# A two-block transformer kernel: rotation products moved to GpSimd, fetches of the second mixer reordered, matmuls in array halves interleaved

## What is computed

```python
h = x + nsa_mixer(rmsnorm(x), ...)          # attention: compressed, selected and windowed keys, 16 heads of 64
h = h + s5_mixer(rmsnorm(h), ...)           # second mixer, below
x = rmsnorm(h, final_norm)
# second block: retention, gated linear attention and sliding-window attention (window 128, 16 heads),
# merged by gates, w_out, then a gated FFN
```

```python
u, z = split(h @ w_in)
x[t] = A * x[t-1] + B @ u[t]                # complex, A = exp(lambda dt), per group
y[t] = Re(C @ x[t]) + d * u[t];  y = gelu(y)
ga, gb = split(y @ w_glu);  out = (ga * sigmoid(gb) * silu(z)) @ w_out
```

## Time and profile before

| | us |
|---|---|
| runs | 2107.24, 2108.03, 2109.11 (median 2108.03) |
| profiled execution, time / span | 2107.77 / 2106.0 |
| TensorE (PE) busy | 1864.1 (89%) |
| DVE busy | 1022.7 (49%) |
| ACT busy | 818.4 (39%) |
| POOL busy | 266.2 (13%) |
| chain that ended last | PE 70%, DVE 17%, ACT 6%, DMA 4%, SP's queue 2% |

### The profile page before, as it was taken

One profiled execution on the slowest core, in us unless ns is written; L12 is line 12 of the kernel. 1 busy time (PEld: TensorE's weight loads), 2 busy tenths in 40 slices (PEclk: granted clock), 3 DMA queues, 4 the chain that ended last, 5 costly groups with the idle time before them and its releaser, 6 DMA issues.

```text
span 2106.0 us, 23601 instructions
## 1 busy us (share of the span) xinstructions
PE 1864.1 (89%) x9454; PEld 1466.5 (70%) x9454; DVE 1022.7 (49%) x1731; ACT 818.4 (39%) x1348; POOL 266.2 (13%) x338
## 2 busy tenths in 40 slices
PE   3478689998976899899799999999999959999996
PEld 2366578776754787687477776887778738888885
DVE  7757855664535436523434544434444354443323
ACT  4024356763213424423434555345542342323222
POOL 0327633540000000000000000012210020111000
PEclk9789899999997999999999999999999979999998
DMA  3153331006774332221132222221122203222331
GB/s 105 66 181 114 103 116 43 12 2 182 175 188 109 117 100 70 100 98 43 40 101 88 80 71 70 93 70 61 51 71 90 90 20 110 92 98 91 99 92 58
DMA packets 80893, 187.56 MB, mean 89 GB/s; under 512 B 24576, under 2 KB 35712, under 8 KB 78992
## 3 DMA queue, kind: packets, MB, share of 16 engines
q1 hardware_dynamic: 80784, 186.06, 28.2%
HBM read 167.68 MB, written 18.35 MB: 88 GB/s over the span
## 4 chain that ended last, share of the span: by engine, by line
PE 70%; DVE 17%; ACT 6%; DMA 4%; SPq 2%; issue 2%; POOL 0%; DVEq 0%; ACTq 0%; POOLq 0%
PE bank L827 17%; PE bank L829 16%; PE bank L828 16%; DVE wlo L1723 2%; PE bank L1008 2%; PE bank L986 2%; PE bank L868 2%; PE bank L866 2%; PE bank L867 2%; PE bank L1199 1%; PE bank L1223 1%; DVE CA L1691 1%; PE bank L847 1%; PE bank L848 1%; PE bank L849 1%
## 5 line engine op out<-in xcount | busy, mean ns | idle before, releaser
L827 PE MATMUL bank<-Hh,whi 128*128 128x512 f32 (+1 forms) x1248 | 503.7, 404 | 27.4 <-DVE wlo L1723 18.2
L828 PE MATMUL bank<-Hl,whi 128*128 128x512 f32 (+1 forms) x1248 | 491.1, 393 | 0.0
L1723 DVE TENSOR_TENSOR wlo<-wraw,whi 128x1024 fp32r<-128x1024 f32 (+1 forms) x262 | 324.2, 1241 | 343.4 <-ACT whi L1250 341.9
L829 PE MATMUL bank<-Hh,wlo 128*128 128x512 f32 (+1 forms) x1248 | 490.9, 393 | 0.0
L1250 ACT ACTIVATE whi<-wraw 128x1024 fp32r<-128x1024 f32 (+1 forms) x262 | 271.2, 1040 | 401.2 <-PE bank L829 273.4
L827 PEld LDWEIGHTS bank<-Hh,whi 128*128 128x128 f32 (+1 forms) x1248 | 236.3, 189 | 92.0 <-DVE wlo L1723 14.8
L829 PEld LDWEIGHTS bank<-Hh,wlo 128*128 128x128 f32 (+1 forms) x1248 | 235.9, 189 | 52.8 <-issue 0.3
L828 PEld LDWEIGHTS bank<-Hl,whi 128*128 128x128 f32 (+1 forms) x1248 | 236.6, 190 | 51.7 <-issue 2.2
L2460 POOL TENSOR_SCALAR bs<-dist 128x256 f32<-128x256 f32 x16 | 7.7, 479 | 900.1 <-DMA dist<-in_c_dist 899.3
L827 PE MATMUL bank<-Bh,whi 128*128 128x512 f32 x256 | 103.7, 405 | 2.2 <-DVE Bl L2253 2.2
L829 PE MATMUL bank<-Bh,wlo 128*128 128x512 f32 x256 | 102.2, 399 | 0.0
(11 more groups left out here) (356 smaller groups left out, 2891.2 us busy)
## 6 DMA issues: line engine op xcount, KB each, us to landing
wraw<-in_w_o SPq DMA_DIRECT2D x24, 512.0 KB, 3.5
wraw<-in_w_bgate SPq DMA_DIRECT2D x24, 512.0 KB, 3.5
wraw<-in_w_branch SPq DMA_DIRECT2D x24, 512.0 KB, 3.5
wraw<-in_w_fg SPq DMA_DIRECT2D x22, 512.0 KB, 3.5
wraw<-in_w_fu SPq DMA_DIRECT2D x22, 512.0 KB, 3.5
wraw<-in_w_s SPq DMA_DIRECT2D x16, 512.0 KB, 3.5
wraw<-in_w_glu SPq DMA_DIRECT2D x16, 512.0 KB, 3.5
wraw<-in_w_fd SPq DMA_DIRECT2D x16, 512.0 KB, 3.5
```

The lines of the kernel that those rows point to most:

```text
L827: pe.matmul(o, wh[:, cols], hi(k), start=k == 0, stop=False)
L828: pe.matmul(o, wh[:, cols], lo(k), start=False, stop=False)
L829: m = pe.matmul(o, wl[:, cols], hi(k), start=False, stop=k == K - 1)
L1723: dve.tensor_tensor(c.wlo[q][:, 0:n], c.raw[i % RR][:, 0:n], c.whi[q][:, 0:n].bitcast(F32), S_).then_inc(*up(DID, ("wlo", i)))
```

## The change

1. The rotations are made on GpSimd (POOL), after attention, in SBUF where they stay (`Rt`, [128, 4, 2, 8, 64]); no DRAM copy, no fetch `mR`. DVE waits for the event `Rt` before the fifth u tile and in `states`. `prep` has six ticks less. The memsets of `kl` no longer stand behind the round trip.
2. Fetches of `mW` (`w`) and of `mCA`/`mT` (`m`) are letters of the order string.
3. The halves of y are made block by block (`y`), in memory of their own (`Yh`, `Yl`); those of the gated result right behind each `glu`.
4. `outputs`: all T matmuls first, before the wait for `Xs`, then all CA matmuls. `gla_o`: all At first, then all St.
5. `rsT` behind the first gemm of the next block, `final_norm` behind the row gemms of `w_rv`.
6. Sliding window: scores of two units are made together, matmuls of the two row halves in turn, in banks of their own; outputs of two units likewise in column halves, one step later; `pTs` has four buffers.

```diff
         self.attention()
+        for m in range(6):
+            self.step("prep_r", m)
         self.pair([("w_o0", 0), ("w_o0", 1)], "g0")
...
-                if b == 0:
-                    self.step("prep_r", n)
-                    yield
-            if b == 0:
-                self.step("prep_rout")
...
-        fns = dict(u=u_tile, r=rows, s=states, o=outputs, t=turned, z=z_tile, f=finish)
-        order = ("u0 u1 r0 u2 u3 r1 s0 u4 u5 r2 o0 s1 u6 u7 r3 t0 o1 s2 z0 z1 f0 t1 o2 s3 z2 z3 f1 t2 o3 z4 f2 t3 z5 "
-                 "z6 z7 f3")
+        def split_y(b):
+            for k in (2 * b, 2 * b + 1):
+                self.step("split_y", k)
+
+        def fetch_w(b):
+            self.step("fetch_w", b)
+
+        def fetch_m(b):
+            self.step("fetch_m", b)
+        fns = dict(u=u_tile, r=rows, s=states, o=outputs, t=turned, z=z_tile, f=finish, y=split_y, w=fetch_w, m=fetch_m)
+        order = ("u0 u1 r0 u2 u3 r1 s0 u4 w1 u5 r2 o0 s1 u6 w2 m2 u7 r3 t0 o1 s2 z0 w3 z1 m3 f0 t1 o2 s3 y0 z2 z3 f1 y1 "
+                 "t2 o3 z4 f2 y2 t3 z5 z6 z7 f3 y3")
         for s in order.split():
             fns[s[0]](int(s[1]))
-        self.step("hold", "y")
-        for k in range(KT):
-            self.step("split_y", k)
+        self.step("hold", "h2")
         self.pair([("w_glu", 0), ("w_glu", 8)], "y")
         for k in range(KT):
...
                 self.gemm("w_r", h, "h2")
-            self.evict(("w_r", h))
-        for h in range(4):
-            self.gemm("w_r", 4 + h, "h2")
-            self.evict(("w_r", 4 + h))
+            if h == 2:
+                self.bank.take("rsT")
+                self.step("rsT")
+                self.bank.give("rsT")
+                self.evict(("w_r", 0))
+                self.evict(("w_r", 1))
+            if h > 1:
+                self.evict(("w_r", h))
         self.rows_v("w_rv")
+        for k in range(KT):
+            self.step("final_norm", k)
         self.side = self.gate_tiles("w_rg")
...
-        for i in range(n + 3):
+        for i in range(n + 4):
+            if i < n and i % 2 == 0:
+                for jj in range(2):
+                    for u in (i, i + 1):
+                        self.bank.take(("ws", u, jj))
+                        self.bank.give(("ws", u, jj))
+                self.step("ws", i)
             if i < n:
-                stage_a(i)
+                self.step("wa", i)
             self.tick()
             if 1 <= i <= n:
                 self.step("wb", i - 1)
-            if i >= 3:
-                stage_d(i - 3)
+            if i >= 4 and i % 2 == 0:
+                self.bank.take(("wo", i // 2 - 2))
+                self.step("wd", i - 4)
+                self.bank.give(("wo", i // 2 - 2))
             if 2 <= i <= n + 1:
-                stage_c(i - 2)
+                for m in range(2):
+                    self.bank.take(("wp", i - 2, m))
...
+        halves = [slice(0, 64), slice(64, 128)]
+        ys = [bank(("y", b, i)) for i in range(2)]
+        for i in range(2):
+            on.wait_ge(*before(plan.bank, ("y", b, i)))
         on.wait_ge(*at("mats", b))
+        for q in range(8):
+            cols = slice((q % 4) * 128, (q % 4) * 128 + 128)
+            for h in range(2):
+                pe.matmul(ys[q // 4][halves[h], cols], c.U[b][:, 2 * q + h, :], T[:, 2 * q + h, :],
+                          start=(q % 4 == 0), stop=False, skip_group_check=True)
         on.wait_ge(*at("xs", b))
-        for i in range(2):
-            y = bank(("y", b, i))
-            on.wait_ge(*before(plan.bank, ("y", b, i)))
-            for q in range(4 * i, 4 * i + 4):
-                cols = slice((q % 4) * 128, (q % 4) * 128 + 128)
-                halves = [slice(0, 64), slice(64, 128)]
+        for q in range(8):
+            cols = slice((q % 4) * 128, (q % 4) * 128 + 128)
+            for part in range(2):
                 for h in range(2):
-                    pe.matmul(y[halves[h], cols], c.U[b][:, 2 * q + h, :], T[:, 2 * q + h, :],
-                              start=True, stop=False, skip_group_check=True)
-                for part in range(2):
-                    for h in range(2):
-                        x = pe.matmul(y[halves[h], cols], c.Xs[b % 2][halves[h], part, q, :],
-                                      CA[halves[h], part, q, 1:9, :].rearrange("p k n -> p (k n)"),
-                                      start=False, stop=(part == 1), skip_group_check=True)
-            x.then_inc(*up(PE, ("y", b, i)))
+                    x = pe.matmul(ys[q // 4][halves[h], cols], c.Xs[b % 2][halves[h], part, q, :],
+                                  CA[halves[h], part, q, 1:9, :].rearrange("p k n -> p (k n)"),
+                                  start=False, stop=(part == 1), skip_group_check=True)
+            if q % 4 == 3:
+                x.then_inc(*up(PE, ("y", b, q // 4)))
 
     def turned(b):
...
+        o = [bank(("go", h, t // 2))[:, (t % 2) * 256:(t % 2) * 256 + 256] for t in range(4)]
         for t in range(4):
-            o = bank(("go", h, t // 2))[:, (t % 2) * 256:(t % 2) * 256 + 256]
             for p in range(2):
-                pe.matmul(o[halves[p], :], c.At[halves[p], t, :], c.gv[halves[p], t, h * 256:h * 256 + 256],
-                          start=True, stop=(t == p == 0), skip_group_check=True)
-            for p in range(2):
-                n = 2 * t + p
-                if n:
-                    on.wait_ge(*at("St", h, n - 1))
-                    x = pe.matmul(o[halves[p], :], q[:, n * 64:n * 64 + 64], c.St[:, n - 1, :],
-                                  start=False, stop=True, skip_group_check=True)
-            if t % 2:
-                x.then_inc(*up(PE, ("go", h, t // 2)))
+                pe.matmul(o[t][halves[p], :], c.At[halves[p], t, :], c.gv[halves[p], t, h * 256:h * 256 + 256],
+                          start=(t % 2 == 0), stop=(t == p == 0), skip_group_check=True)
+        for n in range(1, 8):
+            t, p = n // 2, n % 2
+            on.wait_ge(*at("St", h, n - 1))
+            x = pe.matmul(o[t][halves[p], :], q[:, n * 64:n * 64 + 64], c.St[:, n - 1, :],
+                          start=False, stop=True, skip_group_check=True)
+            if n % 4 == 3:
+                x.then_inc(*up(PE, ("go", h, n // 4)))
 
...
 
-    def wa(u):
-        t, a = u // 2, u % 2
-        half = slice(a * 64, a * 64 + 64)
+    def ws(u):
+        t = u // 2
+        halves = [slice(0, 64), slice(64, 128)]
         on.wait_ge(*at("sq", t))
         on.wait_ge(*at("sk", t // 4))
         for jj in range(2):
-            b = bank(("ws", u, jj))
-            on.wait_ge(*before(plan.bank, ("ws", u, jj)))
+            b = [bank(("ws", u + a, jj)) for a in range(2)]
+            for a in range(2):
+                on.wait_ge(*before(plan.bank, ("ws", u + a, jj)))
             for j in (2 * jj, 2 * jj + 1):
                 k0, W = c.span[j]
                 col = (j % 2) * 256
-                x = pe.matmul(b[:, col:col + W], c.wq[half, t, j * 128:j * 128 + 128], c.wk[half, t // 4, k0:k0 + W],
-                              start=True, stop=True)
-            x.then_inc(*up(PE, ("ws", u, jj)))
+                x = [pe.matmul(b[a][:, col:col + W], c.wq[halves[a], t, j * 128:j * 128 + 128],
+                               c.wk[halves[a], t // 4, k0:k0 + W], start=True, stop=True) for a in range(2)]
+            x[1].then_inc(*up(PE, ("ws", u, jj), ("ws", u + 1, jj)))
 
...
     def wd(u):
-        t, a = u // 2, u % 2
-        g = 2 * (t // 4) + a
+        t = u // 2
         o = bank(("wo", t))
-        if a == 0:
-            on.wait_ge(*before(plan.bank, ("wo", t)))
-        on.wait_ge(*at("pTs", u, 0))
-        on.wait_ge(*at("pTs", u, 1))
+        on.wait_ge(*before(plan.bank, ("wo", t)))
+        for i in range(2):
+            on.wait_ge(*at("pTs", u, i))
+            on.wait_ge(*at("pTs", u + 1, i))
         on.wait_ge(*at("w_sv"))
         for n, (j, k) in enumerate(c.blocks):
             nb, kt = c.span[j][1] // 128, c.span[j][0] // 128 + k
-            x = pe.matmul(o[a * 64:a * 64 + 64, j * 128:j * 128 + 128], c.wv[:, kt, g * 64:g * 64 + 64],
-                          c.pTs[u % 2][:, n, :], start=(k == 0), stop=(k == nb - 1), skip_group_check=True)
-        x.then_inc(*up(PE, ("wd", u)))
+            for a in range(2):
+                g = 2 * (t // 4) + a
+                x = pe.matmul(o[a * 64:a * 64 + 64, j * 128:j * 128 + 128], c.wv[:, kt, g * 64:g * 64 + 64],
+                              c.pTs[(u + a) % 4][:, n, :], start=(k == 0), stop=(k == nb - 1), skip_group_check=True)
+        x.then_inc(*up(PE, ("wd", u), ("wd", u + 1)))
...
         on.wait_ge(*at("inv", "h1"))
+        if k == 4:
+            on.wait_ge(*at("Rt"))
         dve.tensor_tensor(r(dst), r(bank(key)), c.rs[:, :].rearrange("p (n s) -> p s n", s=8), M).then_inc(
             *up(DID, ("u", k) if k < 8 else ("zraw", k - 8), ("freed", key)))
 
     def states(b):
```

(39 more changed lines are left out.)

107 lines of the change are left out of this document (35 added, 72 removed).

## The result

| | before | after |
|---|---|---|
| median of runs, us | 2108.40 | 2048.44 (2043.19 to 2053.46, 4 runs) |
| profiled execution, time / span, us | 2107.77 / 2106.0 | 2053.18 / 2051.4 |

The account below looks back on a forecast made before the run. TensorE, busy 89% of the span, was taken as the bound. Terms −18 + 1 − 40.5 − 5.5 − 6 − 3.7 − 27 = −99.7 took 2107.8 to 2008 us; range 1994 to 2031, the terms' ends adding to −72 and −124.

Parts of the forecast that it names:

- Part 1, first mixer: Rotations off DVE in the first mixer: TensorE's later waits for DVE's work shrink, −18 us, between −27 and −13.
- can begin it in the 14.6 us: First mixer: DVE's side work, due six ticks earlier, fills the 14.6 us in which DVE idles before 150.2.
- TensorE's waits before 300 at half: Sign for the first mixer: TensorE's waits before 300 us would fall to half.
- Part 2, POOL: Rotations on POOL behind attention: 31 us, hidden, but slowing DVE through shared SBUF, +1 us, from 0 to +3.
- DVE waits more than it works there: Behind attention, 473 to 510 us: the reason given for taking only +1 us for POOL's slowing of DVE.
- Part 3, second mixer: Second mixer: no wait for the rotations' fetch, w_glu's gemm at 670 instead of 710.65, −40.5 us, from −27 to −46.
- W3 is issued at 620.9: Second mixer: the fourth block's mW fetch goes out at 620.9, behind mCA and mT, and lands about 627.4.
- mW late: Rival, second mixer: mW fetches take 11.4 us or DVE's wlo slips, −27 instead of −40.5, 2021 us; 15 in 100.
- Part 4: After the second mixer: waits for zyr and wlo fall away, clock gains 0.6, −5.5 us; rst's wait filled, −6.
- Part 5: Gated linear attention: all At first, then all St, saves 6 switches of form in each of 4 heads, −3.7 us.
- Part 6, sliding window: Sliding window: a pair of units' scores or outputs costs what one unit costs, −27 us, from −20 to −28.
- all of it counts: Sliding window: TensorE is the bound, so the whole −27 us shortens the time unless the wait behind takes it.

Follow-up runs that it names:

- eight ticks more: Changed kernel with eight more ticks of side work between the first mixer's cmp_w1 gemms, two a step instead of one: 2039.1 us.
- ticks put back: Changed kernel with the six ticks that the rotations had in the first mixer's side work put back as empty ticks: 2047.9 us.
- no rotations: Changed kernel with the 38 rotation operations on GpSimd left out and Rt filled with zeros by one memset: 2040.0 us.
- the changed kernel again: The changed kernel itself, unaltered, run once more as the measure for the other runs: 2047.0 us, ratio 0.9710 to the kernel before.
- old order in outputs and gla_o: Changed kernel with T and CA, and At and St, in turn again as in the kernel before: 2049.8 us.
- the unpaired run: Changed kernel with the sliding window as before, no pairs in scores and outputs and two buffers pTs: 2065.4 us.

## Why the prediction was wrong

**Part 1, first mixer: the step that DVE "can begin it in the 14.6 us", −18, failed.** It gave −11.4. I took time that DVE no longer works for time that the queue can use. The freed 21.6 us lay where DVE's queue stood at operations that wait for ACT: the idle stretch of 14.6 us went, but two of 6.6 and 5.7 opened, and those of 4.3 and 4.6 grew to 9.3 and 10.4. The run with eight ticks more shows it: side work in front of those operations gives 12.6 us more at the end of attention. That the six ticks matter was wrong too (ticks put back). The sign "TensorE's waits before 300 at half" did not come either: without the first weight load they fell from 46.8 to 32.7 us.

**Part 2, POOL: the mechanism was right, +1 should have been +5.3 net.** POOL's own time was 37 us (461.6 to 498.9) instead of 31, hidden as forecast. I measured what sharing does to DVE by POOL's spread, 1.8 times; DVE's operations with two inputs in SBUF stretched 1.6 to 4.1 times. And "DVE waits more than it works there" looked at an average: the last 16 us of POOL fell on the seven operations between X and TensorE's fourth tile. They cost TensorE 7.9 us (no rotations).

**Part 3, second mixer: the step "W3 is issued at 620.9" failed.** The sum was −40.5, measured −19.9. The time of each fetch was about right (8.3, 5.5, 7.7 us; 6.3 to 6.5 in the walk), the time of its issue was not. In the forecast's frame (6.1 us added, the lead at states(0)) W1 went out at 574.0, W2 at 598.9 and W3 at 631.9, against 573.5, 594.9 and 620.9. I put W3 behind a weight load, mCA and mT only; the rows of U and the round trip of y stand on SP in front of it as well, each with a landing that the next one waits for. Of the 20.6 us that are missing, 12.2 are there when states(3) starts (639.6 instead of 627.4). Of the rest, 1.5 are states(3) itself, 3.5 us instead of 2.0 at a granted clock of 0.54, and 5.1 are two waits of TensorE, 4.2 for wlo and 0.9 for `Yo`: in the trace gelu and the halves of the third block stand on ACT in front of that weight split and wait for y's round trip, which wasn't tried by itself. The last 1.8 are not assigned. The rival "mW late" named the fetch and its sign, but by the transfer's length, −27; it was the queue. w1, w2 and w3 ahead of the round trips bring 9 us back, 11.5 in the trace.

**Part 4.** The wait for zyr went, one of 1.9 us for wlo stayed, and the granted clock was 0.99 instead of 0.96: −3.8 instead of −5.5. rst: −6.6 instead of −6, as its wait fell from 6.8 to 1.3 us. The 1.9 us lost in retention are the granted clock of that one execution (see the changed kernel again).

**Part 5** was right, −3.6, and o took 5.6 us, 5.4 worked out: 14 fewer changes of form saved 2.0 us, 0.14 each, and 6 fewer in each of the four heads 3.7, 0.15 each. The Trainium skill, TensorEngine Tiling (Array Packing), Key Properties, says that a change of tiling mode drains the array; the trace agrees in that each change costs time. In the second mixer the wait for mW took all of it (old order in outputs and gla_o).

**Part 6, sliding window: the price of a pair was right to 0.1 us, the step "all of it counts" failed.** Between the first scores and the last outputs TensorE's work fell by 26.4 us, from 160.7 to 134.3, where 27 were forecast; the time fell by 15.8, as TensorE's waits grew from 1.3 to some 12 us. (The 24.5 in the expectation of the unpaired run is too low.) I looked for what is late next at POOL's slack, and missed that softmax closes on itself at 8.8 us a unit: DVE waits for the bias. The trace of before had its first signs, 2.6 us in three waits for it, and POOL's queue with the bias behind the normalising.

The three large misses (parts 1, 3 and 6) have one form: a gain was priced by what was in the way then, not by the second bound just behind it. The end of the range, 2031, left too little for it, as the misses had a common form and added up. The sum of the terms' ends was wrong too: by the terms as they stand it is −66 and −122, not −72 and −124. The measured −60 lies outside both. And the wait for zyr and the 1.8 for wlo give 4.7, with 0.6 for the clock 5.3, not 5.5.

## What to carry to other kernels

Where work leaves an engine, look at what stands at the head of its queue in the time that is freed; if that waits for others, move the rest in front of it, or nothing moves. Walk a DMA queue with the landing of each item that the next one waits for, not with issue times, and put a fetch that needs nothing ahead of round trips. Before counting a gain at the bound engine in full, close the loop through the other engines for one period: if two of them wait for each other, the period can't fall below theirs.

## What the runs showed that was not expected

VectorE beside GpSimd, both working in SBUF on fp32: DVE's split of 1024 elements took 2.9 us instead of 1.2, a sum of 512 2.78 instead of 0.68, while a sum of 512 with one input in PSUM stayed at 0.67; GpSimd's operations on 1024 took 2.2 to 3.3 us. Scores and outputs of two units in halves of the array took what one unit takes, 1.79 and 1.75 us against 1.78 and 1.74, over eight pairs, but for one pair of outputs behind a wait of 2.4 us, which took 3.26. And behind a stall of 15 us the matmuls of the states took 3.53 us at a granted clock of 0.54, mostly the lower of TensorE's two levels (1.2 GHz), against 2.09 in a busy stretch at 1.00 (2.4 GHz).
